# Values stand in attention's products and probabilities move; GpSimd divides by the sums; modulated tokens are made beside the value stage

## What is computed

```python
a = rms_norm(h, norm_mix[l])
(q_na, k_na, v_na, q_hg, z_f, z_b, i_hg, g_hg, gate_na, gate_hg) = split_cols(a @ w_in[l])
...
s_win = jnp.einsum('brchd,brjwhd->bhrcjw', qg, k_blk).astype(jnp.float32) * scale
s_win = jnp.where(in_win[:, None, :], s_win + bias[None], -1e30)
s_meta = jnp.einsum('brchd,bmhd->bhrcm', qg, km).astype(jnp.float32) * scale
s = jnp.concatenate([s_win.reshape(B, H, rows, GRID_W, kh * GRID_W), s_meta], axis=-1)
p = jax.nn.softmax(s, axis=-1).astype(v.dtype)
o_grid = (jnp.einsum('bhrcjw,brjwhd->brchd', p_win, v_blk)
          + jnp.einsum('bhrcm,bmhd->brchd', p_meta, vm)).reshape(B, T, H, dh)
```

## Time and profile before

| | us |
|---|---|
| Median of 3 runs | 872.39 |
| Lowest and highest | 870.58, 873.76 |
| The profiled execution's own time | 876.36 |
| Span of the profiled execution, first to last instruction | 874.6 |
| Mean granted clock of TensorE in it | 0.991 of full speed |
| Busy: TensorE, VectorE, ScalarE, GpSimd | 842.2, 628.8, 489.0, 102.0 |

### The profile page before, as it was taken

One profiled execution on the slowest core, in us unless ns is written; L12 is line 12 of the kernel. 1 busy time (PEld: TensorE's weight loads), 2 busy tenths in 40 slices (PEclk: granted clock), 3 DMA queues, 4 the chain that ended last, 5 costly groups with the idle time before them and its releaser, 6 DMA issues.

```text
span 874.6 us, 16326 instructions
## 1 busy us (share of the span) xinstructions
PE 842.2 (96%) x6576; PEld 805.6 (92%) x6576; DVE 628.8 (72%) x1009; ACT 489.0 (56%) x869; POOL 102.0 (12%) x122
## 2 busy tenths in 40 slices
PE   5899999999998999999999989999999999999996
PEld 4879879998998999999999889999997999999995
DVE  5746658992899878787799686776788548455663
ACT  6434446663656646473666653554577457566541
POOL 0000046320112000000030420000202030000001
PEclk9999999999999999999999999999999999999998
DMA  9833433453468897979778455555655436555431
GB/s 356 295 96 97 141 111 117 136 169 121 137 223 282 307 377 244 378 250 380 250 238 297 156 169 167 172 190 195 190 156 172 132 105 200 178 150 159 147 101 48
DMA packets 47385, 170.35 MB, mean 195 GB/s; under 512 B 5200, under 2 KB 6480, under 8 KB 47056
## 3 DMA queue, kind: packets, MB, share of 16 engines
q1 hardware_dynamic: 46592, 165.31, 57.1%
q10 hardware_dynamic: 720, 4.01, 1.2%
HBM read 168.26 MB, written 1.05 MB: 194 GB/s over the span
## 4 chain that ended last, share of the span: by engine, by line
PE 79%; DVE 11%; ACT 4%; issue 3%; DMA 2%; SPq 0%; POOL 0%; POOLq 0%; DVEq 0%; ACTq 0%
PE bank L183 79%; DVE wl L222 4%; DMA h<-in_xt 2%; DVE raw L210 1%; DMA raw<-in_ws 1%; ACT wh L192 1%; DVE B1l L210 1%; DVE h L210 1%; DVE XAl L222 0%; ACT B1h L189 0%; DVE B0l L222 0%; ACT L198 0%; DVE A L210 0%; ACT sq L189 0%; PE bank L186 0%
## 5 line engine op out<-in xcount | busy, mean ns | idle before, releaser
L222 DVE TENSOR_TENSOR wl<-raw,wh 128x1024 fp32r<-128x1024 f32 x259 | 326.5, 1272 | 22.8 <-ACT wh L192 22.3
L192 ACT CAST wh<-raw 128x1024 fp32r<-128x1024 f32 x259 | 268.8, 1047 | 113.7 <-PE bank L183 57.0
L183 PE MATMUL bank<-XAh,wl 128*128 128x256 f32 (+1 forms) x896 | 257.5, 287 | 1.4 <-DVE wl L222 1.3
L183 PE MATMUL bank<-XAh,wh 128*128 128x256 f32 (+1 forms) x896 | 251.5, 281 | 0.0
L183 PE MATMUL bank<-XAl,wh 128*128 128x256 f32 (+1 forms) x896 | 251.5, 281 | 0.0
L183 PEld LDWEIGHTS bank<-XAh,wl 128*128 128x128 f32 x896 | 170.0, 190 | 3.8 <-issue 1.7
L183 PEld LDWEIGHTS bank<-XAl,wh 128*128 128x128 f32 x896 | 170.2, 190 | 0.0
L183 PEld LDWEIGHTS bank<-XAh,wh 128*128 128x128 f32 x896 | 169.6, 189 | 0.1
L183 PE MATMUL bank<-B1h,wl 128*128 128x256 f32 (+1 forms) x464 | 131.8, 284 | 3.0 <-DVE B1l L210 3.0
L183 PE MATMUL bank<-B1h,wh 128*128 128x256 f32 (+1 forms) x464 | 130.7, 282 | 0.0
L183 PE MATMUL bank<-B1l,wh 128*128 128x256 f32 (+1 forms) x464 | 130.6, 282 | 0.0
(11 more groups left out here) (260 smaller groups left out, 1190.1 us busy)
## 6 DMA issues: line engine op xcount, KB each, us to landing
raw<-in_ws SPq DMA_DIRECT2D x307, 512.0 KB, 4.4
bias<-in_bias ACTq DMA_DIRECT2D x1, 1664.0 KB, 9.4
hK<-in_xk SPq DMA_DIRECT2D x4, 272.0 KB, 5.2
h<-in_xt ACTq DMA_DIRECT2D x1, 1088.0 KB, 15.1
out<-h SPq DMA_DIRECT2D x4, 256.0 KB, 2.5
C<-in_cst SPq DMA_DIRECT2D x1, 512.0 KB, 8.2
crow<-in_crow ACTq DMA_DIRECT2D x1, 512.0 KB, 17.2
wT<-in_wt SPq DMA_DIRECT2D x1, 512.0 KB, 6.9
```

The lines of the kernel that those rows point to most:

```text
L183: return self.real.matmul(*a, **k)
L192: return self.real.copy(*a, **k)
L222: return self.real.tensor_tensor(*a, **k)
```

## The change

- **Queries in pairs.** `q` leaves `ALONE`: two tiles share a bank, and only the 256 grid tokens are multiplied, as two runs of 128 columns (`both_halves`), where it was 272 with the meta tokens between.
- **Tokens later.** `scaled` waits eight steps in place of four, so its pieces are made in the v stage. There and after it the side list holds `scaled` and `attention` in turns, with two steps a unit: one for each in v. `attention` has 24 steps in place of 28.
- **Values stand.** The product with the values has the values as the standing operand (64 columns) and the transposed probabilities moving (128 columns). The result has channels in the partitions, so that the transposes `na_turn`, the tile `oN` and its division by the sums go. `B0h` and `B0l` are read out of the bank of `pv`.
- **Division earlier, on GpSimd.** After the sums' reciprocal (VectorE, into `nmr`) GpSimd multiplies the 128 x 416 exponentials of the head (`prob`), and the transposes wait for that in place of `exp`. VectorE's reciprocals come a step earlier, right after the scores of their head where it can.
- **Loads.** ScalarE issues `h`, `bias`, `negw` after `rsqrt` and in this order, and `crow` at the start of the v stage.

```diff
-        ALONE = ("k", "q", "zf", "a", "qk", "glr")
+        ALONE = ("k", "zf", "a", "qk", "glr")
...
+                of, cols = (in_halves, both_halves) if X is XU else (lambda x: x, lambda x: x[:, n0:n0 + 256])
...
-                            m = three(tile(label, t), (hi[:, k, s], lo[:, k, s]),
-                                      (X[0][:, xk + q + k, n0:n0 + 256], X[1][:, xk + q + k, n0:n0 + 256]),
+                            m = three(of(tile(label, t)), (hi[:, k, s], lo[:, k, s]),
+                                      (cols(X[0][:, xk + q + k, :]), cols(X[1][:, xk + q + k, :])),
                                       opens and q + k == 0 and b == 0, ends and q + k == nk - 1 and b == 1, True)
...
-            w.side.append(scaled(8))
-            XU = (XUh, XUl)
+            scaling = scaled(12)
+            w.side.append(scaling)
             t_tiles("k", "w_in", 512, 1024, XU, unnormed("mix"), lambda t: [("kT", t)], n1=272)
-            t_tiles("q", "w_in", 0, 512, XU, unnormed("mix"), lambda t: [("qT", t)], n1=272)
+            t_tiles("q", "w_in", 0, 512, XU, unnormed("mix"), lambda t: [("qT", t)])
...
-                        for b in range(2):
-                            e.wait_ge(*at("exp", (s - 1, b)))
+                        e.wait_ge(*at("prob", s - 1))
...
+                        po = 64 * (hh % 2)
                         for b in range(2):
-                            o = bk("pv", hh // 2)[:, 128 * b + 64 * (hh % 2):128 * b + 64 * (hh % 2) + 64]
-                            z = slice(0, 80) if b else slice(64, 112)
-                            e.matmul(o, PT[hh % 2][:, 128 * b:128 * b + 128], vN[:, b, vs], start=True, stop=False)
-                            m = e.matmul(o, PTm[hh % 2][z, 128 * b:128 * b + 128], vM[z, vs], start=False, stop=True)
+                            o = bk("pv", hh // 2)[po:po + 64, 128 * b:128 * b + 128]
+                            z, n = slice(0, 80) if b else slice(64, 112), slice(128 * b, 128 * b + 128)
+                            e.matmul(o, vN[:, b, vs], PT[hh % 2][:, n], start=True, stop=False)
+                            m = e.matmul(o, vM[z, vs], PTm[hh % 2][z, n], start=False, stop=True)
                         m.then_inc(*up("pv", hh))
                         if hh % 2:
-                            side.give(("pv", hh // 2), ("out_nat", hh // 2))
+                            side.give(("pv", hh // 2), ("na_high", hh // 2), ("na_low", hh // 2))
                         yield
-                    if s >= 4 and s % 2 == 0:
-                        p = s // 2 - 2
-                        ps = side.take("na_turn", p)
-                        e.wait_ge(*at("out_nat", p))
-                        for b in range(2):
-                            m = e.transpose(ps[:, 128 * b:128 * b + 128], oN[p % 2][:, 128 * b:128 * b + 128],
-                                            cst_("ident"))
-                        m.then_inc(*up("na_turn", p))
-                        side.give(("na_turn", p), ("na_high", p), ("na_low", p))
-                        yield
-
-            w.side.append(attention())
-            w.steps = 1
+
+            w.side[:] = [in_turn(scaling, attention())]
+            w.steps = 2
...
+            rsqrt("mix", bk("sums", "mix")[:, 0:272], 272, ("sums", ("mix", 6)), rsK)
+            e.dma_start(h[:, :, :], xt).then_inc(one["h"], 16)
             e.dma_start(bias[:, :, :], biasd).then_inc(one["bias"], 16)
             e.dma_start(negw[:, :], negwd).then_inc(one["negw"], 16)
-            e.dma_start(h[:, :, :], xt).then_inc(one["h"], 16)
-            e.dma_start(crow[:, :], crd).then_inc(one["crow"], 16)
-            rsqrt("mix", bk("sums", "mix")[:, 0:272], 272, ("sums", ("mix", 6)), rsK)
 
             def scaled():
-                for _ in range(4):
...
-                    if 2 <= s <= 9:
-                        yield
-                    if s >= 4 and s % 2 == 0:
-                        p = s // 2 - 2
-                        e.wait_ge(*at("na_turn", p))
-                        e.copy(by_eights(B0h[:, p, :]), eights(bk("na_turn", p)[:, 0:256])).then_inc(
-                            *up("na_high", p))
+                    if s >= 2:
+                        if s % 2:
+                            p = s // 2 - 1
+                            e.wait_ge(*at("pv", s - 2))
+                            e.copy(by_eights(B0h[:, p, :]), eights(bk("pv", p)[:, 0:256])).then_inc(*up("na_high", p))
                         yield
...
-            w.side.append(attention())
-            w.steps = 1
+            w.side[:] = [in_turn(scaling, attention())]
+            w.steps = 2
+            e.dma_start(crow[:, :], crd).then_inc(one["crow"], 16)
...
-                        for _ in range(4):
+                        for _ in range(8):
...
             def q_out(ts):
                 for t in ts:
                     e.wait_ge(*at("mm", ("q", t)))
-                    ps, rs = (x[:, 0:288].rearrange("p (b n) -> p b n", b=2)[:, :, 0:128] for x in (bk("q", t), rsK))
-                    e.scalar_tensor_tensor(qT[:, t, :, :], ps, 0.125, rs, ALU.mult, ALU.mult).then_inc(*up("qT", t))
-
-            w.side.append(scaled())
+                    e.scalar_tensor_tensor(qT[:, t, :, :], in_halves(tile("q", t)), 0.125, both_halves(rsK), ALU.mult,
+                                           ALU.mult).then_inc(*up("qT", t))
...
-                    e.reciprocal(shr[hh // 2 % 2][:, :, hh % 2], nmr[hh % 3][:, 2:4]).then_inc(*up("share", hh))
+                    e.reciprocal(nmr[hh % 3][:, 4:6], nmr[hh % 3][:, 2:4]).then_inc(*up("share", hh))
...
+                        if s == 1:
+                            share(0)
...
-                        if s - 1 >= 4:
-                            e.wait_ge(*at("out_nat", (s - 1) // 2 - 2))
-                        share(s - 1)
+                        if s < 8:
+                            share(s)
                         yield
-                    if 2 <= s <= 9:
+                    if s >= 2:
                         yield
                         if s % 2:
                             p = s // 2 - 1
-                            e.wait_ge(*at("pv", s - 2))
-                            e.wait_ge(*at("share", s - 2))
-                            if p >= 2:
-                                e.wait_ge(*at("na_turn", p - 2))
-                            e.tensor_tensor(oN[p % 2][:, :].rearrange("p (a c) -> p a c", c=64),
-                                            bk("pv", p)[:, 0:256].rearrange("p (a c) -> p a c", c=64),
-                                            bc(flat(shr[p % 2][:, :, :]), [[1, 4], [0, 64]]), ALU.mult).then_inc(
-                                                *up("out_nat", p))
-                    if s >= 4 and s % 2 == 0:
-                        p = s // 2 - 2
-                        yield
-                        e.wait_ge(*at("na_high", p))
-                        e.tensor_tensor(by_eights(B0l[:, p, :]), eights(bk("na_turn", p)[:, 0:256]),
-                                        by_eights(B0h[:, p, :].bitcast(F32)), ALU.subtract).then_inc(*up("na_low", p))
-
-            w.side.append(attention())
-            w.steps = 1
+                            e.wait_ge(*at("na_high", p))
+                            e.tensor_tensor(by_eights(B0l[:, p, :]), eights(bk("pv", p)[:, 0:256]),
+                                            by_eights(B0h[:, p, :].bitcast(F32)), ALU.subtract).then_inc(
+                                                *up("na_low", p))
+
+            w.side[:] = [in_turn(scaling, attention())]
+            w.steps = 2
...
+            scaling = scaled(12)
+            w.side.append(scaling)
             tiles("k", "w_in", 512, 1024)
             tiles("q", "w_in", 0, 512)
 
-            w.side.append(scaled(28))
-            w.steps = 1
+            def attention():
+                def shares(hh):
+
+                    S = sP[hh % 3][:, :].rearrange("p (b n) -> p b n", b=2)
+                    e.wait_ge(*at("share", hh))
+                    e.tensor_tensor(S, S, bc(nmr[hh % 3][:, 4:6], [[1, 2], [0, 208]]), ALU.mult).then_inc(
+                        *up("prob", hh))
+
+                for s in range(10):
+                    if s < 8:
+                        if s == 1:
+                            shares(0)
+                        yield
+                    if 1 <= s <= 8:
+                        if s < 8:
+                            shares(s)
+                        yield
+                    if s >= 2:
+                        yield
+
+            w.side[:] = [in_turn(scaling, attention())]
+            w.steps = 2
             rows("v", "w_in", 1024, 1536)
```

27 lines of the change are left out of this document (16 added, 11 removed).

## The result

| | before | after |
|---|---|---|
| Median of 20 runs each, side by side | 874.89 us | 869.97 us |
| Lowest and highest | 870.58, 877.82 | 868.62, 871.83 |
| Ratio after/before, 95% interval | | 0.9952 [0.9938, 0.9965] |
| Profiled execution's span | 874.6 | 869.8 |

The medians differ by 4.9 us, the ratio is 4.2 us of 874.89, and the spans differ by 4.8. The forecast was 7.1 us less, 865.3, within 862.0 to 869.8. The time lies just outside the range. The sign was right, the size was not.

What follows compares the result with a forecast made beforehand. TensorE, busy 842.2 of 874.6 us, was taken as the bound, with its waits. Gains 4.0 + 0.6 + 1.1 + 1.6 + 0 - 0.2 = 7.1 us took the median 872.39 to 865.3, range 862.0 to 869.8.

Steps and rivals of the forecast that it cites:

- The stall and its slow clock: Before and in the value stage: the 2.5 us wait for `qT` goes, and 1.5 us of half-speed clock with it.
- 256 columns: Query stage: 96 matmuls of 256 in place of 272 columns save 0.6 us, with 0 as the lower bound.
- Output transposes and `oN` waits: Attention: four pairs of output transposes go, 1.1 us, and TensorE's waits for `oN` with them, 1.6 us.
- Values stand. I take no change: Attention's value products: turning the operands costs nothing; bounds 2.3 us less and 3.2 us more in all.
- the recurrence's level: Comparison for value products: eight instructions, 128 columns moving and 128 standing, take 0.81 us, 0.10 each.
- Division on GpSimd: Attention: eight operations at 1.3 us, up to 2.3; 0.2 us lost at the last head, up to 1.0.
- The columns of the products are not hidden: Rival, attention's value products: 64 further moving columns cost 3.2 us, gain 3.9, time 868.5; chance 0.12.
- The standing columns bound the products: Rival, attention: a head's value products fall to 0.81 us, 2.3 us more gain, 9.4 in all, 863.0; chance 0.06.
- The estimate from the Trainium skill: Value products: two loads of 64 columns fewer each, 3.4 us over 32 products if no load were hidden; sum 10.5.
- The other rivals: Division on the path, 869.1, chance 0.12; another stall at zf, 869.3, 0.08; GpSimd shutting out VectorE, 881.5, 0.04.

Runs made afterwards that it cites:

- The interleaved heads: Changed kernel with the value products of a pair's two heads in turn, reordered, three buffers of turned probabilities: median 866.34 us, ratio 0.9896 to the kernel before.

## Why the forecast was right and wrong

- **The stall and its slow clock, 4.0: right in size, half right in cause.** Measured 3.00 - 0.33 + 1.54 = 4.2, and with the stall of 3.2 us that the kernel before had in its second profile it would have been more. The forecast named both VectorE's order and the two banks. It did not see that either suffices. With the pairs in place the tokens' and loads' moves won nothing measurable in Q, V or A.
- **256 columns, 0.6: too much.** Measured 0.33, above the lower bound 0: a matmul of q takes 0.120 us from start to start, where the forecast took the 0.118 of the zb stage.
- **Output transposes and `oN` waits, 1.1 + 1.6: a little too small.** With the probabilities standing and these gone A is 52.93, 3.07 us less than before; 2.7 were forecast, and 0.2 less for GpSimd.
- **"Values stand. I take no change": this is the step that failed.** Measured 1.87 us more, 52.93 to 54.80, inside its bounds of -2.3 and +3.2: 1.29 in the products and the transposes ahead of them, 0.36 in the units' last matmuls ahead of them, and 0.2 in pace, which no run ties to the operands. The argument compared with the recurrence's level, eight alike loads of 128*128 in a row at 0.10 us, and concluded that streaming 128 columns is not the limit. Two things were wrong with that. The forecast wrote that the pieces of 48, 128 and 80 rows "stay" without asking what halving the standing columns adds: two more changes of the load's shape a head, at about 0.1 us each. And between such changes the moving columns do cost: beside 128 standing ones, 1.0 us over the eight heads.
- **Division on GpSimd, 0.2 lost: right**, and nothing lost at all.
- **The sum.** 4.2 + 0.3 + 3.1 - 1.9 = 5.7, and at stage i the changed kernel is 5.6 ahead. The remaining difference to 4.2 to 4.9 has two candidates: the 0.94 us behind the stop, and how often each kernel's executions have the shorter stretch from 271 to 455. Neither is shown to be the change's.
- **The base.** 865.3 was 7.1 less than a median of three runs, 872.39, of which two lay in the lower group of the kernel's times. Over 20 runs the median is 874.89; 7.1 less would have been 867.8, and the corrected 5.7 gives 869.2 against 869.97. If the seven lower times of the kernel before are executions with the shorter stretch, which is shown for one profiled execution (870.53) alone, like is compared with like in the median of its other thirteen, 875.9: an estimate of 5.9 us for the gain.
- **Rivals.** "The columns of the products are not hidden" came closest, in its kind and its sign, with 1.0 where it had 3.2. "The standing columns bound the products" was wrong: the eight instructions went from 1.10 to 1.31 us. The estimate from the Trainium skill, TensorE: Matmul & The Clock Gate, "LDWEIGHTS (loading the stationary operand)", held only if no load were hidden. The rows of loads agree with this page of the Trainium skill (two loads of 64 columns take 0.19 us, of 128 columns 0.30, and 48 rows as long as 128), but loads of one shape were hidden. The other rivals left no trace: no wait for `sP` or `XAl` up to 130 us.

The same page of the Trainium skill, "The mechanism" in its Part 3, has in its list loads overlap running products only where the row groups differ; its paragraph before also allows it for a load into a background buffer. The list doesn't fit the rows here: loads of one shape are hidden, and those that change rows or columns mostly are not. That page of the Trainium skill also says that products in different tiles of the array overlap, with the column tile set by where the output starts ("What picks the tile position"). The interleaved heads agree with it, 1.17 us for a pair against 2.25.

## What to carry to other kernels

Before you turn a product's operands round, write down the shapes of successive weight loads, not only the columns that move: each change of shape cost about 0.1 us, and between such changes more moving columns cost as well. Order the pieces so that like shapes follow each other. Two small products whose results go to different halves of the partitions ran in the time of one when they alternated; what fed them then came late, so look again at every wait once a part has become shorter. And judge a change of half a per cent by stretches of the trace that repeat to a tenth, after checking that the base itself isn't one of two groups.

## What was not expected

- Two heads of products, alternating between the two halves of the result's partitions, took 1.17 us for 16 instructions; the same one head after the other, 2.25.
- One kernel, unaltered, ran 352 or 342 matmuls of 256 columns in the same 40 us, at the full granted clock in both; in that kernel it came to 5.2 us.
- A wait of 1.5 us in the fastest kernel cost 3.1, as the granted clock fell to 0.50 behind it; waits of 0.4 and 0.9 at about the same place, in two other kernels, left it at 1.00.
- The half-clock time behind one and the same stop of 3.9 us was worth 1.7 or 3.4 us of clock time, in one kernel both.
- GpSimd's multiplication of 128 x 416 took 0.88 or 1.78 us and nothing between.
